# One attention loop written out, its weight loads shifted, and matrix powers turned instead of multiplied

## The reference, cut to what matters

```python
def dilated_attention_mixer(h, positions, w_in, w_out):
    proj = (h @ w_in).reshape(B, S, N_DIL_GROUPS, 3, A_HEADS, A_HEAD_DIM)
    for gi, (window, dil) in enumerate(DILATED_GROUPS):
        q = (rotary(proj[:, :, gi, 0], positions) * scale)
        k = rotary(proj[:, :, gi, 1], positions)
        o, lse = dilated_window_attention(q, k, v, window, dil)
    ...
def gated_delta_rule(q, k, v, g, beta):      # in chunks
    lower = jnp.where(strict, jnp.einsum('bhnid,bhnjd->bhnij', kb, k) * decay, 0.0)
    a_mat = lower + jnp.eye(C)
    sol = lax.linalg.triangular_solve(a_mat, rhs, ...)   # inverse of a_mat applied
    ...
def modulate(x, c, w_ada, b_ada):
    shift, scale, gate = jnp.split(c @ w_ada + b_ada, 3, axis=-1)
```

## Time and profile before

| | |
|---|---|
| time, median of 3 runs | 2637.5 us |
| time of the profiled execution | 2632.27 us |
| its span | 2630.6 us |
| PE busy | 2466.9 us (94%) |
| PE weight load busy | 1446.6 us (55%) |
| DVE busy | 1206.1 us (46%) |
| ACT busy | 590.5 us (22%) |
| POOL busy | 492.6 us (19%) |
| DMA | 657.49 MB, mean 250 GB/s |
| mean granted TensorE clock | 0.979 |

### The profile page before, as it was taken

One profiled execution on the slowest core, in us unless ns is written; L12 is line 12 of the kernel. 1 busy time (PEld: TensorE's weight loads), 2 busy tenths in 40 slices (PEclk: granted clock), 3 DMA queues, 4 the chain that ended last, 5 costly groups with the idle time before them and its releaser, 6 DMA issues. The chain is left out here.

```text
span 2630.6 us, 39106 instructions
## 1 busy us (share of the span) xinstructions
PE 2466.9 (94%) x14213; PEld 1446.6 (55%) x14214; DVE 1206.1 (46%) x2562; ACT 590.5 (22%) x1359; POOL 492.6 (19%) x488
## 2 busy tenths in 40 slices
PE   5999999999999999999997999999899999999996
PEld 3878778786854333333334668476764433333332
DVE  3846567584344333323236544545443333333326
ACT  1132131413121111111113333333211111111111
POOL 2504224150011111111100212222001111111110
PEclk9999999999999999999998999999999999999998
DMA  7726335363468999999965131221628999999967
GB/s 252 209 73 189 116 113 161 88 198 109 175 242 322 388 411 418 417 412 406 419 242 195 46 100 47 77 67 45 228 101 333 360 413 417 415 420 412 402 269 291
DMA packets 173637, 657.49 MB, mean 250 GB/s; under 512 B 25300, under 2 KB 87100, under 8 KB 118296
## 3 DMA queue, kind: packets, MB, share of 16 engines
q1 hardware_dynamic: 117936, 409.57, 40.8%
q10 hardware_dynamic: 20280, 136.27, 13.0%
q0 software_dynamic: 35248, 109.36, 12.0%
HBM read 616.27 MB, written 53.52 MB: 255 GB/s over the span
## 5 line engine op out<-in xcount | busy, mean ns | idle before, releaser
L1726 DVE TENSOR_SCALAR core_oT<-moe_tx,moe_by,moe_plus 128x128 f32<-128x128 f32 x360 | 123.0, 404 | 549.5 <-PE moe_tx L1991 549.3
L2016 PE MATMUL moe_ph<-weights_w,core_oT 128*32 128x512 f32 (+2 forms) x1216 | 309.3, 614 | 7.8 <-issue 7.8
L2030 PE MATMUL moe_py<-weights_w,moe_hT 128*32 128x512 f32 (+2 forms) x1296 | 312.7, 596 | 0.9 <-ACT moe_hT L1446 0.9
L1525 POOL DMA_INDIRECT y_rows<-moe_ysb,moe_yidx x90 | 102.2, 1136 | 930.5 <-DVE moe_idx L1718 562.9
L2016 PE MATMUL moe_pr<-weights_w,core_oT 128*64 128x512 f32 (+2 forms) x864 | 271.1, 597 | 0.2 <-issue 0.2
L1446 ACT COPY moe_hT<-moe_th 128x256 f32<-128x256 f32 x90 | 33.6, 373 | 917.4 <-PE moe_th L1979 917.4
L2659 PE MATMUL gdn_pj<-core_hT,core_ring 128*128 128x512 f32 x512 | 226.5, 596 | 5.2 <-ACTq L2393 5.1
L2659 PEld LDWEIGHTS gdn_pj<-core_hT,core_ring 128*128 128x128 f32 x512 | 96.8, 191 | 122.5 <-issue 122.5
L2030 PEld LDWEIGHTS moe_py<-weights_w,moe_hT 128*32 128x32 f32 (+2 forms) x1296 | 92.4, 128 | 120.6 <-issue 113.3
L2016 PEld LDWEIGHTS moe_pr<-weights_w,core_oT 128*64 128x64 f32 (+2 forms) x864 | 91.3, 140 | 111.1 <-issue 110.5
L2016 PE MATMUL moe_ph<-core_ring,core_oT 128*32 128x512 f32 (+2 forms) x512 | 144.9, 608 | 4.4 <-issue 4.4
(11 more groups left out here) (455 smaller groups left out, 4185.0 us busy)
## 6 DMA issues: line engine op xcount, KB each, us to landing
weights_w<-in_expert_w_dram SPq DMA_DIRECT2D x160, 1024.0 KB, 14.4
weights_w<-in_expert_w_dram ACTq DMA_DIRECT2D x92, 1024.0 KB, 10.4
core_ring<-in_expert_w_dram SPq DMA_DIRECT2D x54, 1024.0 KB, 14.3
core_hT<-in_expert_w_dram SPq DMA_DIRECT2D x48, 1024.0 KB, 13.5
core_ring<-in_attn_w_in_dram SPq DMA_DIRECT2D x36, 1024.0 KB, 5.9
weights_w<-y_rows SPq DMA_DIRECT2D x32, 1024.0 KB, 12.8
core_ring<-in_expert_w_dram ACTq DMA_DIRECT2D x30, 1024.0 KB, 10.0
attn_ada_w<-in_ada_w_dram POOLq DMA_DIRECT2D x64, 384.0 KB, 4.0
```

The costliest lines, as they stand in the source:

```text
L1525: pool.indirect_dma_start(y_rows, bass.IndirectOffsetOnAxis(ap=yidx[:, s:s + 1], axis=0), ysb[:, b], None, bounds_check=SEQ * TOPK - 1, oo ...
L1726: last = nc.vector.tensor_scalar(xT[:, b, k], tx[1][:, k - 4], by[:, k:k + 1], plus[:, k:k + 1], ALU.mult, ALU.add)
L2016: last = nc.tensor.matmul(ph[p % 2][at, :], xT[:, p % 2, k, at], w13[ew.up_place(n)[0]][:, :, k], start=k == 0, stop=k == KT - 1)
L2030: last = nc.tensor.matmul(py[n][at, :], hT2[:, p % 2, k, at], w2[ew.down_place(m)[0]][:, k, half(n)], start=k == 0, stop=k == 1)
```

## The change

It has four parts.

1. PE's attention program is no longer a loop: all four turns are written out.
2. In the first turn `product_2(0, 0)` stands right behind `product_1(0, 0)` and no longer between `product_5` and `product_3`; `product_7(0, 0)` waits for three of the four token differences instead of all four.
3. GpSimd's side loads that belong to VectorE's first two steps behind a sub-chunk move past the next `add_up`.
4. In the DeltaNet, Q (the transposed power) is made by turning the P that ScalarE copied, not by a second product. P and Q get semaphores of their own.

```diff
@@ GpSimd, attention
-                    for _ in range(min(BETWEEN + BEHIND[s] + (ada.slots if s == 0 else 0), ada.steps - j)):
+                    far = sum(BEHIND[0:s]) + BETWEEN * (s + 1) + ada.slots + max(BEHIND[s] - BETWEEN, 0)
+                    for j in range(j, min(far, ada.steps)):
                         ada.load(pool, i, j)
-                        j += 1
+                    j = min(far, ada.steps)
@@ TensorE, attention
                             product_5(i, 0)
-                            product_2(i, 0)
+                            if i:
+                                product_2(i, 0)
                             product_3(i, 0)
...
             product_1(0, 0)
+            product_2(0, 0)
             pe.wait_ge(toks_ready, 2)
             product_6(0, 0)
+            pe.wait_ge(toks_ready, 3)
+            product_7(0, 0)
             pe.wait_ge(toks_ready, 4)
-            product_7(0, 0)
             product_4(0, 0)
-            with pe.Fori(0, QUADS - 1) as i:
-                quad(i, True)
-            quad(QUADS - 1, False)
+            for i in range(QUADS):
+                quad(i, i + 1 < QUADS)
@@ ScalarE, DeltaNet
                     for h in range(HP):
                         act.wait_ge(pw_done[s], 2 * i + h + 1)
+                        nc.scalar.copy(pd[h][:], ps[h][1][:]).then_inc(pw_ready[s], 1)
+                    for h in range(HP if qd is not None else 0):
+                        act.wait_ge(q_done[s], 2 * i + h + 1)
                         if s == 1:
                             act.wait_ge(E_first, 2 * i + h + 1)
-                        last = nc.scalar.copy(pd[h][:], ps[h][1][:])
-                        if qd is not None:
-                            last = nc.scalar.copy(qd[h][:], ps[h][2][:])
-                        last.then_inc(pw_ready[s], 1)
+                        nc.scalar.copy(qd[h][:], ps[h][2][:]).then_inc(q_ready[s], 1)
@@ TensorE, DeltaNet
-                    each(ps[h][1], lambda t: Q0[h][:, t], lambda t: P0[h][:, t])
-                    each(ps[h][2], lambda t: P0[h][:, t], lambda t: Q0[h][:, t]).then_inc(pw_done[0], 1)
+                    each(ps[h][1], lambda t: Q0[h][:, t], lambda t: P0[h][:, t]).then_inc(pw_done[0], 1)
...
                         pe.wait_ge(pw_ready[s], n)
                         if s < 2:
-                            last = each(ps[h][1], lambda t: q[h][:, t], lambda t: p[h][:, t])
-                            if s == 1:
-                                last.then_inc(pw_done[2], 1)
+                            turn(ps[h][2], p[h], q_done[s])
                         if s == 0:
-                            each(ps[h][2], lambda t: p[h][:, t], lambda t: q[h][:, t]).then_inc(pw_done[1], 1)
                             pe.wait_ge(qk_ready, n)
                         pe.wait_ge(ready, n)
                         each(ps[h][0], lambda t: p[h][:, t], lambda t: e[h][:, t]).then_inc(e_done[s], 1)
+                    if s < 2:
+                        for h in range(HP):
+                            pe.wait_ge(q_ready[s], 2 * i + h + 1)
+                            each(ps[h][1], lambda t: q[h][:, t], lambda t: p[h][:, t]).then_inc(pw_done[s + 1], 1)
```

More of the change, by code:

```diff
@@ L2332, in delta_stage @@
     pw_ready = [sem(f"pw_ready{n}") for n in range(3)]
+    q_done = [sem(f"q_done{n}") for n in range(2)]
+    q_ready = [sem(f"q_ready{n}") for n in range(2)]
     e_done = [sem(f"e_done{n}") for n in range(6)]
```

## The result

The change makes the kernel slower: 2659.8 us (median of 4 runs, 2656.98 to 2660.19) against 2636.0 (4 runs), a ratio of 1.0082 with a 95% interval of 1.0067 to 1.0096. Predicted were 2619.0, with a range of 2612 to 2627. (A fourth run of the kernel before moved its median from 2637.5 to 2636.0.)

The account below looks back on a forecast made before the run. TensorE was taken to bound attention and DeltaNet, so its stream and idle time count. Gains of 7.5 + 0 + 4.4 + 6.5 = 18.4 us from the median 2637.5 gave 2619.0 us, range 2612 to 2627.

Parts of the forecast that it names:

- What bounds the kernel: Attention and DeltaNet: TensorE's stream or idle time in it decides; what a mixer gains stays, since MoE loads follow its end.
- Part 1: First two attention turn changes: holes of 3.28 and 2.90 us go, both come down to 3.9 us, gain 7.5 us.
- ScalarE's turn-back: Rival at attention turn changes: ScalarE's own loop branch becomes the new wait, gain only 4.3, total 2622.2 us; chance 13%.
- What is late next: Attention turn changes without holes: ScalarE's 1.28 us table load ahead of product 3's copy, making 3.9 us, not 3.6.
- Part 2: First attention chunk: product 2 fills a 1.65 us idle, but product 3 then waits about 1.9; net 0.
- Part 3: Attention: TensorE's six waits for GpSimd's sums go, 4.4 us gained; ends 0 and 5.
- No wait, then, at the median landing: Sub-chunk 3, turn 3: VectorE's join comes 2 us later, yet product 2 keeps 0.6 to 0.7 us to spare.
- some 2 us earlier ..., 532.3: Turn 3: first load behind the second pair of sums, now load 5, goes out at 532.3 instead of 534.37.
- GpSimd's sums no longer run while VectorE joins, so its joins and rotations get shorter: Attention: argument against the rival that side loads give back what the sums gain; no size given.
- Part 4: DeltaNet powers: transposes replace second products, 1.82 less 0.2 of waits, 1.6 us a turn, 6.5 in four.
- the fourth: Rival, attention: side loads landing late behind the second pair of sums delay the join; slower, about 2670 us; chance 3%.
- the second rival: Attention: side loads give back what the sums gain, the late join leaving 0 of 4.4 us, total 2623.4; chance 11%.

Follow-up runs that it names:

- experiment 3: The kernel before with only TensorE's attention program written out, nothing else changed: 2632.6 us, ratio 0.9991 to the kernel before.
- experiment 6: The changed kernel with 7, 15, 19, 23 side loads ahead of GpSimd's sums, so the first boundary as before, later ones two later: 2644.5 us, ratio 1.0029.
- experiment 1: The changed kernel with GpSimd's old order of side loads put back, all else kept: 2625.3 us, ratio 0.9964 to the kernel before.

## Why the prediction was wrong

**What bounds the kernel: right, with a gap.** The MoE kept its length (765.0, 765.2), and what the mixers lost stayed lost. But "there a microsecond counts if it is a microsecond of TensorE's stream" left out that VectorE and its side loads run only just ahead of it. The earlier trace rows named GpSimd in all six waits; I took them for an effect of the queue order alone.

**Part 1: right at its place, wrong in what it brings.** The changes came down to 3.81 us each, for 8.5 and 6.8: 7.7 us, for 7.5 forecast. ScalarE's turn-back fits into the 1.50 us for which ScalarE waits for product 5 anyway (the row at 213.52); at TensorE's price it would have made the step 5.3 us or more. Less than 1.5 us cannot be told from nothing here. But the attention gained only 0.5 us with three slots (experiment 3). "What is late next" has to be asked for the sums too, not only for ScalarE's table load.

**Part 2: right.** First product to values, 30.60 us before (43.02 to 73.62) and 30.32 after (42.38 to 72.70), with the wait of 1.84 before product 3 as forecast.

**Part 3: the step that failed.** The gain of 4.4 for GpSimd's waits was as argued; they went. What failed is the price of the chain behind it, "No wait, then, at the median landing": it was priced with 0.7 us to spare, and two of its terms were off, the start of load 5 and the length from there to the join. In turn 3, on the clock of before:
- "some 2 us earlier ..., 532.3": load 5 went out at 555.66 - 20.82 = 534.8, 2.5 us later. The sums ahead of it could not start earlier: they waited 8.76 us for their weights. The trace of before would have told it, since there the weights landed only 0.2 us ahead of the sums. Two loads fewer ahead of sums that wait for a transfer win nothing, and load 5 pays for the sums.
- From that load to the join I had 552.7 - 532.3 = 20.4 us; it took 579.40 - 555.66 = 23.7. 2.45 of the 3.3 are the last two steps, 4.52 us instead of 2.07, since the sums of the next sub-chunk start two loads sooner and run beside them (575.44). The rest, 0.9, is about what the longer landings make (4.3 for 4.0, 1.1 by the prediction's own sum, which had said that a wait begins at 4.2).
- Together they make the join 5.9 us later than I wrote, and with 0.7 to spare that makes a wait of 5.2. The row has 5.09.

I also did the sum for one join in three. The later boundaries cost 19.2 us by themselves (experiment 6), since steps 15, 19 and 23 stand ahead of the rotation as step 5 does. And "GpSimd's sums no longer run while VectorE joins, so its joins and rotations get shorter" had the wrong sign where it counts: the sums left work that the swap transfer hid and met work behind it.

**Part 4: right.** 1.70 us a turn for 1.6 forecast, 5.7 to 7.2 by the stage, 7.9 by the medians. By an estimate from the Trainium skill's 275 ns for one bfloat16 transpose ("TensorE: Matmul & The Clock Gate", Part 4: PE-mode transpose) it would have been a loss of 3.3 us; the trace does not agree, four transposes step by 0.44 us.

**The rivals.** What happened is the fourth, which I gave 3%: its place (product 2 of sub-chunk 3 waiting for the join) is right, its condition wrong. The waits at product 2 are also the sign that I had named for the second rival (11%), which priced them at 4.4 us where they and what hangs on them took 38. I let the fourth decide by a mean landing of 5.5 us. The medians after are 4.1 to 4.4 in the four turns; in turn 3, beside 3.4/4.0/7.4 in the earlier trace rows:

```profile
DMA to landing us min/median/max: 3.4/4.3/6.5
```

What came late was the start of the chain; the lower end of part 3 in the range was 0. The total, +23.8 for a forecast of -18.4, is off by 42 us: by the experiments with one part each, 38 of them are part 3 (+33.5 for -4.4), and 4 are part 1's gain, which the waits took (-3.5 for -7.5).

## What to carry to other kernels

When an instruction is moved behind another in a queue, ask what its new predecessor waits for and how long it runs: here the sums waited for a weight transfer and could not start earlier, and a load whose slot was free stood 7.4 us behind them. Of every load, find the first consumer that has something urgent queued behind it; one load later was free, two cost 1.3% of the kernel: the second fed a step ahead of the rotation, and the sums moved with it. And if two engines slow each other, moving one of them moves the slowdown too: look at what hides the work that it meets there. Holes taken from the bounding engine pay only as far as its helpers have slack, so buy that slack (a fourth buffer) in the same change.

## What the runs showed of the hardware

- VectorE and GpSimd elementwise work on float32 slow each other: VectorE's pair of writes of q takes 1.96 us alone and 3.90 beside GpSimd's sums, its pair of swap multiplies 1.28 and 3.83; GpSimd's L706 takes 1.28 and 1.98. Not every VectorE instruction is slowed. After the change, turn 1, while GpSimd's L706 ran from 260.10 for 1.98 us and L708 from 262.04 for 1.44:

```profile
261.20 0.41 DVE L751 TENSOR_TENSOR attn_raw<-attn_u,attn_sc 128x256 f32<-128x256 f32 x1
261.53 0.82 DVE L753 TENSOR_TENSOR attn_raw<-attn_u,attn_m 128x256 f32<-128x256 f32 x1
262.46 1.57 DVE L761 TENSOR_TENSOR attn_rot<-attn_raw,attn_w_cos 128x512 f32<-128x512 f32 x1
```

  The part of the join that reads `attn_sc`, a PSUM bank, keeps its 0.41 us; the next, of the same shape with both inputs in SBUF, takes 0.82, and L761 takes 1.57 where it has 0.69 alone. The Trainium skill ("SBUF — State Buffer", SBUF: two separate sides) says that VectorE and GpSimd share one port pair, which a VectorE instruction with two SBUF inputs takes against GpSimd for its whole length. The trace agrees on which instructions are slowed: the one with an input in PSUM is not, the two with both inputs in SBUF are.
- TensorE's clock after an idle stretch: a group of 8 records takes 1.89 us at a granted clock of 1.00 and 3.78 at the 0.50 that follows a wait of 3.60 us. The attention's loss against experiment 1 is 31.4 us, the idle time for joins and sums only 21.5 more (30.5 for 9.0). The rest is in the records themselves: the same 3689 of them are busy for 602.2 us after and for 592.9 in experiment 1. They lie behind the waits: the first groups behind each of the ten, counted as above against 1.73 us a group, take 13.8 us more in sum, 0.1 to 3.1 each.
